# Attention outputs and gates of a fused transformer stretch by token instead of by feature, with a turn per tile

## The chip, the cores and the metric

One core of one Trainium2 chip runs the whole kernel in one launch. The metric is the device time in microseconds, as the median of three runs. A core has TensorE (matrix products, results in PSUM), VectorE, ScalarE, GpSimd and SyncE (here the queue that issues the loads), each with its own instruction stream; they meet at semaphores.

## The reference, cut to what matters

A batch of one, 256 tokens, width 2048, all in float32. First a layer with two token mixers, whose results are gated and added, then a feed-forward net; then two more layers (a pooling layer and a sparse attention layer), each with a small attention to a memory. The parts that the change touches:

```
# token mix
o = gla_chunked(q, k, v, log_a)                       # 4 heads, 512 values each
o = rmsnorm(o, gla_onorm_g) * silu(p_g)               # over the 512 of a head
y_gla = o @ gla_wo                                    # 2048 x 2048
y_mla = o_m @ mla_wo                                  # 2048 x 2048
merged = sigmoid(p_ga) * y_gla + sigmoid(p_gb) * y_mla
out = merged @ w_out
# pool layer
mixed = einsum('bsgc,gcd->bsgd', pooled, w_pool)      # 4 groups, 384 x 384
y_pool = mixed * scale * silu(zu)
y_mem = memory_attention(qm, mem, ...) * silu(zm)     # 4 heads
x + concatenate([y_pool, y_mem]) @ w_out
```

p_g, p_ga and p_gb are slices of h @ w_in, 2048 columns each.

## The kernel before

**Products.** Every large product runs as tiles of 512 output columns by 256 tokens. A tile needs its 2048 inputs in four pieces of weights (1 MB each, four chunks of 128 input rows by 512 columns). A piece is loaded into one of four w_raw buffers by SyncE's queue, which waits until the piece four places earlier has been used (free_slot). ScalarE rounds it to fp32r in two halves (w_hi, L1427), VectorE subtracts to get the rest (w_lo, L1843, also in two halves); the two together are called a cut. The cut of a piece may start when TensorE is done with the piece two places earlier, since there are two w_hi and two w_lo. TensorE then makes three passes, w_hi with x_hi, w_lo with x_hi, w_hi with x_lo (L945).

**Two modes.** In mode T the weights are stationary (128 x 128 blocks) and the 256 tokens move: the result stands by feature, [128 features, chunks, 256 tokens], and a piece is 48 matmuls of 256 columns. In mode N the tokens are stationary (two blocks of 128) and 512 weight columns move: the result stands by token, [128 tokens, 2, 512], and a piece is 24 matmuls of 512 columns. A product's input must stand by feature in either mode. Before, gla_g, gate_a, gla_wo, gate_b and mla_wo are in mode T; w_out, both parts of the feed-forward net and gla_v are in mode N.

**Order.** Each engine's stream is written out by its own product() calls, in the order gla_g, gate_a, gla_wo, mla_cq, mla_ckv, mla_kr, gate_b, the softmax attention, mla_wo, w_out. PSUM has two tile buffers (tile_ps) that alternate, and two for other work (misc_ps). A tile is emptied by ScalarE or VectorE (its "take"); this is held back and issued after the cut of the second piece of the next tile (or at the product's end). The list `between` gives extra steps, one after each piece. Products with rider=2 also carry the matrix ada_w: after each two pieces comes one ada piece, for which VectorE does four operations of 128x512 (L1914), and after two tiles TensorE sums them with eight matmuls. A piece of ada stands on VectorE ahead of the cut of the third and of the fifth piece from a tile's start. A product with several turns is a hardware loop on TensorE and SyncE, or has its first turn written out (peel), or is written out whole (flat).

**Around the linear attention.** Its output (gla_output, L1254) goes by feature into tile_ps[0], ScalarE copies it to qk (head_out, L1709). After the last head ScalarE squares all four heads, TensorE sums the squares over the features with 32 matmul instructions against ones (gla_sums), VectorE scales them, ScalarE takes the root, and VectorE the reciprocals of 128x1024 values in two steps (L2284). For each gla_g tile ScalarE makes Silu into gla_tmp, and VectorE (gated) multiplies four chunks by gain and reciprocal, multiplies by gla_tmp, and splits into o_hi and o_lo. gate_a becomes merged, gla_wo's take multiplies into it. mla_wo's take (both_merge) is four operations of 128x1024 on VectorE: times gate_b, plus merged, cast to h_hi, subtract to h_lo.

**The feed-forward net** already has the turn that the change brings elsewhere: a tile pair's result stands by token in o_tmp, eight transposes on TensorE (L1322) put it by feature into misc_ps[0], ScalarE rounds it, VectorE makes the low part.

**The pool stage.** pool_w has four pieces of three chunks by 384 columns, one per tile, cut over all 2048 columns of the buffer. The take of a tile (pool_take, L2439) makes three products, a cast and a subtraction on VectorE. The memory attention has nine steps over four units; the first three stand between the pieces of pool_w, the other six between those of pool_out, whose order has piece four of the first tile late. TensorE waits for all four takes before pool_out.

## Time and profile before

| | us |
|---|---|
| median of 3 runs (lowest, highest) | 2879.85 (2878.52, 2881.31) |
| the profiled execution | 2880.43 |
| its span, first to last instruction | 2878.6 |
| TensorE matmul busy | 2756.4 (96%) |
| VectorE busy | 1766.1 (61%) |
| ScalarE busy | 1220.8 (42%) |
| mean granted TensorE clock | 0.983 |

Busy times are of instructions, which overlap on TensorE: the spacing of two starts is shorter than the time of one matmul. Where starts are subtracted below, it is this spacing that counts.

### The profile page before, as it was taken

How to read it: one execution, taken by the hardware profiler on the slowest of the kernel's cores; microseconds unless marked ns; L12 is line 12 of the kernel's file. 1: busy time of each engine (PE TensorE's matmuls, PEld its weight loads, DVE VectorE, ACT ScalarE, POOL GpSimd, SP SyncE). 2: the span in 40 equal slices, each digit the busy share in tenths (PEclk: the TensorE clock that was granted, in tenths of full speed). 3: DMA queues.
4: the chain of work that ended last, by engine and by line, in shares of the span. 5: the costliest groups of instructions: out<-in, count | busy, mean ns of one | idle time of the engine just before them, and what ended most of it. 6: DMA issues, size and time to landing. Idle time of an engine off the chain costs nothing.

```text
span 2878.6 us, 41377 instructions
## 1 busy us (share of the span) xinstructions
PE 2756.4 (96%) x17422; PEld 2484.6 (86%) x17422; DVE 1766.1 (61%) x2132; ACT 1220.8 (42%) x1628; POOL 10.9 (0%) x21
## 2 busy tenths in 40 slices
PE   8989989999999999999999999999998999899998
PEld 6878878999999879888888888888997799899876
DVE  7866787767665567764445544456546556645765
ACT  6445433333434433444443343444443444434554
POOL 0000000000000000000000000000000000000000
PEclk9989999999999999999999999999999999999999
DMA  9987805877777247755555555554554545555233
GB/s 340 367 284 262 293 34 181 292 268 270 228 259 191 93 138 261 284 190 187 192 187 191 198 192 187 205 192 138 188 176 156 186 147 183 181 183 161 89 109 126
DMA packets 316861, 574.84 MB, mean 200 GB/s; under 512 B 22399, under 2 KB 61639, under 8 KB 315288
## 3 DMA queue, kind: packets, MB, share of 16 engines
q1 hardware_dynamic: 314034, 561.56, 57.4%
q0 software_dynamic: 2192, 10.77, 1.1%
q8 instruction: 122, 2.00, 0.3%
q14 instruction: 43, 0.35, 0.0%
q10 hardware_dynamic: 470, 0.16, 0.0%
HBM read 568.24 MB, written 4.21 MB: 199 GB/s over the span
## 4 chain that ended last, share of the span: by engine, by line
PE 82%; DVE 11%; DMA 3%; ACT 3%; issue 2%; SPq 0%; ACTq 0%; DVEq 0%
PE tile_ps L945 75%; PE misc_ps L945 6%; DVE w_lo L1843 4%; DMA w_raw<-in_w_mem_kv 2%; ACT w_hi L1427 1%; DVE probs_t L1914 1%; DVE probs_t L1934 1%; DMA w_raw<-in_w_in 1%; DVE strip_wide L1934 1%; PE misc_ps L1113 1%; PE misc_ps L1322 0%; DVE stats L2134 0%; DMA w_raw<-in_ada_w 0%; ACT mem_t L1640 0%; DVE gla_var L2284 0%
## 5 line engine op out<-in xcount | busy, mean ns | idle before, releaser
L1843 DVE TENSOR_TENSOR w_lo<-w_raw,w_hi 128x1024 fp32r<-128x1024 f32 x866 | 1020.9, 1221 | 903.9 <-ACT w_hi L1427 902.8
L1427 ACT ACTIVATE w_hi<-w_raw 128x1024 fp32r<-128x1024 f32 x866 | 868.6, 1051 | 1209.9 <-PE tile_ps L945 1150.7
L945 PE MATMUL tile_ps<-h_hi,w_hi 128*128 128x256 f32 x2544 | 429.6, 290 | 34.1 <-DVE w_lo L1843 18.8
L945 PE MATMUL tile_ps<-h_hi,w_lo 128*128 128x256 f32 x2544 | 420.3, 286 | 0.0
L945 PE MATMUL tile_ps<-h_lo,w_hi 128*128 128x256 f32 x2544 | 420.0, 286 | 0.0
L945 PEld LDWEIGHTS tile_ps<-h_hi,w_hi 128*128 128x128 f32 x2544 | 360.7, 195 | 42.1 <-issue 23.4
L945 PEld LDWEIGHTS tile_ps<-h_lo,w_hi 128*128 128x128 f32 x2544 | 359.3, 195 | 0.0
L945 PEld LDWEIGHTS tile_ps<-h_hi,w_lo 128*128 128x128 f32 x2544 | 359.2, 195 | 0.0
L945 PE MATMUL tile_ps<-w_hi,h_hi 128*128 128x512 f32 x1056 | 329.0, 393 | 5.4 <-DVE w_lo L1843 4.6
L945 PE MATMUL tile_ps<-w_lo,h_hi 128*128 128x512 f32 x1056 | 325.8, 390 | 0.0
L945 PE MATMUL tile_ps<-w_hi,h_lo 128*128 128x512 f32 x1056 | 325.7, 390 | 0.0
L945 PEld LDWEIGHTS tile_ps<-w_hi,h_hi 128*128 128x128 f32 x1056 | 196.8, 188 | 46.5 <-DVE w_lo L1843 6.2
L945 PEld LDWEIGHTS tile_ps<-w_lo,h_hi 128*128 128x128 f32 x1056 | 198.5, 188 | 41.7
L945 PEld LDWEIGHTS tile_ps<-w_hi,h_lo 128*128 128x128 f32 x1056 | 198.5, 188 | 41.6
L1914 DVE SCALAR_TENSOR_TENSOR probs_t<-w_raw,c_act,probs_t 128x512 f32<-128x512 f32 x240 | 180.1, 750 | 6.9
L945 PE MATMUL tile_ps<-w_hi,sw_hi 128*128 128x512 f32 x352 | 108.6, 390 | 0.0
L945 PE MATMUL tile_ps<-w_lo,sw_hi 128*128 128x512 f32 x352 | 108.4, 389 | 0.0
L945 PE MATMUL tile_ps<-w_hi,sw_lo 128*128 128x512 f32 x352 | 108.3, 389 | 0.0
L945 PE MATMUL tile_ps<-w_hi,o_hi 128*128 128x512 f32 x256 | 81.1, 398 | 10.7 <-DVE o_lo L1980 9.1
L945 PE MATMUL tile_ps<-o_hi,w_hi 128*128 128x256 f32 x512 | 83.9, 287 | 5.4 <-DVE w_lo L1843 4.2
L945 PE MATMUL tile_ps<-o_hi,w_lo 128*128 128x256 f32 x512 | 83.5, 286 | 0.0
L945 PE MATMUL tile_ps<-o_lo,w_hi 128*128 128x256 f32 x512 | 83.1, 285 | 0.0
(370 smaller groups left out, 2816.8 us busy)
## 6 DMA issues: line engine op xcount, KB each, us to landing
w_raw<-in_w_in SPq DMA_DIRECT2D x89, 1024.0 KB, 5.0
w_raw<-in_ffn_w_in SPq DMA_DIRECT2D x88, 1024.0 KB, 4.9
w_raw<-in_ada_w SPq DMA_DIRECT2D x80, 1024.0 KB, 5.1
w_raw<-in_w_out SPq DMA_DIRECT2D x48, 1024.0 KB, 5.1
w_raw<-in_ffn_w_down SPq DMA_DIRECT2D x44, 1024.0 KB, 5.0
w_raw<-in_b_w_in SPq DMA_DIRECT2D x33, 1024.0 KB, 5.3
w_raw<-in_a_w_in SPq DMA_DIRECT2D x32, 1024.0 KB, 5.3
w_raw<-in_w_kv SPq DMA_DIRECT2D x24, 1024.0 KB, 5.0
```

What stands on the lines that cost most here:

```text
L945: return nc.tensor.matmul(o, l, r, start=start, stop=stop, skip_group_check=True)
L1113: last = nc.tensor.transpose(bank[2][0:k, a * P:(a + 1) * P], probs_of(name, u0 + e)[:, hd * nk + j * P:hd * nk + j * P + k], ident)
L1427: f(w_hi[s_ % 2][:, hf], w_raw[r % 4][:, hf], ACT.Copy).then_inc(cut_hi, 1)
L1843: ins = v.tensor_tensor(w_lo[s_ % 2][:, hf], w_raw[r % 4][:, hf], f32(w_hi[s_ % 2][:, hf]), ALU.subtract)
L1914: ins = v.scalar_tensor_tensor(acc, w[:, c, :], c_act[:, k:k + 1], acc, ALU.mult, ALU.add)
L1934: ins = v.scalar_tensor_tensor(acc, w[:, c, :], c_act[:, k:k + 1], acc, ALU.mult, ALU.add)
```

## The change

Five products go to mode N, two of them flat. The linear attention's output is made by token, and its mean square comes from ScalarE as it empties PSUM. The gate (without the gain) is applied by token in place; each head is then turned back by eight transposes into misc_ps[0], where ScalarE (four operations with the gain as scale) and VectorE (four) make o_hi and o_lo. Both merges work by token; mla_wo's sum is turned back per tile in the same way, with one operation on each engine behind it. The turn of the last head or tile stands in the next product. In the pool stage the attention steps all stand in pool_out, in six groups of 2, 2, 2, 1, 1, 1; pool_out waits for each take where its chunk needs it; and a cut covers only the columns in use.

```diff
-            Product("gla_g", 4, 4, rider=2), Product("gate_a", 4, 4, rider=2),
-            Product("gla_wo", 4, 4, rider=2),
+            Product("gla_g", 4, 4, mode="N", rider=2, flat=True), Product("gate_a", 4, 4, mode="N", rider=2),
+            Product("gla_wo", 4, 4, mode="N", rider=2),
...
-            Product("gate_b", 4, 4, rider=2)]
+            Product("gate_b", 4, 4, mode="N", rider=2)]
...
-PRODUCTS += [Product("mla_wo", 4, 4, rider=2), Product("w_out", 4, 4, mode="N", rider=2)]
+PRODUCTS += [Product("mla_wo", 4, 4, mode="N", rider=2, flat=True), Product("w_out", 4, 4, mode="N", rider=2)]
...
+        MEM_A_GROUPS = (2, 2, 2, 1, 1, 1)
+        def in_next_tile(steps, at_, last_at):
+            out = [None] * BLK
+            for do in steps[:-1]:
+                out += [None] * at_ + [do] + [None] * (BLK - 1 - at_)
+            return out, [None] * last_at + [steps[-1]]
+        def halves(s_):
+            n = USED[s_] // 2
+            return slice(0, n), slice(n, 2 * n)
...  TensorE: linear attention output, sums, turns
-                for c in range(BLK):
-                    v = slice(hd * GLA_DV + c * P, hd * GLA_DV + (c + 1) * P)
-                    mm(tile_ps[0][:, c * S:(c + 1) * S], gla_v[:, 0, v], att[:, 0:2, :], c % 2 == 0, False)
-                    last = mm(tile_ps[0][:, c * S + P:(c + 1) * S], gla_v[:, 1, v], att[:, 2, :], False, True)
+                mm(tile_ps[0][:, 0:NT], att[:, 0, :], gla_v[:, 0, cs], True, True)
+                mm(tile_ps[0][:, NT:], att[:, 1, :], gla_v[:, 0, cs], True, False)
+                last = mm(tile_ps[0][:, NT:], att[:, 2, :], gla_v[:, 1, cs], False, True)
-            product("gla_g", *h, peel=True, between=[lambda: (pe.wait_ge(gl_out, GLA_H), gla_sums())])
+            def turn_tile(src, into):
+                for c in range(BLK):
+                    for tt in range(TT):
+                        last = nc.tensor.transpose(into[:, c * S + tt * P:c * S + tt * P + P],
+                                                   src[:, tt, c * P:c * P + P], ident)
+                return last
+            def turn_head(hd):
+                pe.wait_ge(gl_gated, TT * hd + TT)
+                if hd:
+                    pe.wait_ge(gl_ready, hd)
+                turn_tile(o_rows[:, hd], misc_ps[0]).then_inc(gl_turned, 1)
+            woven, last = in_next_tile([lambda hd=hd: turn_head(hd) for hd in range(GLA_H)], 0, 0)
+            product("gla_g", *h, between=woven)
+            product("gate_a", *h, between=last, peel=True)
+            product("gla_wo", *o, chunk_ready=lambda k: [(gl_ready, k // BLK + 1)] if k % BLK == 0 else [])
...
+            def turn_merged(tb):
+                pe.wait_ge(wo_merged, tb + 1)
+                if tb:
+                    pe.wait_ge(wo_ready, tb)
+                turn_tile(mla_tmp[:], misc_ps[0]).then_inc(wo_turned, 1)
+            woven, last = in_next_tile([lambda tb=tb: turn_merged(tb) for tb in range(BLK)], 1, 1)
+            product("mla_wo", *o, ready=fin("mla1"), between=woven)
...  ScalarE
+                for tt in range(TT):
+                    act.wait_ge(nm_sq, N["gla"].a0 + TT * hd + tt)
+                    f(sq_out[:], tile_ps[0][:, tt * NT:(tt + 1) * NT], ACT.Square,
+                      accum_out=row_sq[:, 0, tt, hd:hd + 1]).then_inc(nm_sq, 1)
+                f(o_rows[:, hd], tile_ps[0][:].rearrange("p (a b) -> p a b", a=TT), ACT.Copy).then_inc(gl_out, 1)
...
+            def head_high(hd):
+                act.wait_ge(gl_turned, hd + 1)
+                for c in range(BLK):
+                    f(o_hi[:, BLK * hd + c, :], misc_ps[0][:, c * S:(c + 1) * S], ACT.Copy,
+                      scale=vec("gla_onorm_g", c)).then_inc(gl_high, 1)
+            woven, last = in_next_tile([lambda hd=hd: head_high(hd) for hd in range(GLA_H)], 1, 1)
+            product("gla_g", silu_g, between=[gla_root] + woven[1:])
...  VectorE
+                for tt in range(TT):
+                    o_ = o_rows[:, hd, tt, :]
+                    v.scalar_tensor_tensor(o_, o_, row_sq[:, 1, tt, hd:hd + 1], gla_tmp[:, hd % 2, tt * NT:(tt + 1) * NT],
+                                           ALU.mult, ALU.mult).then_inc(gl_gated, 1)
...
-                step(i, tb, g, 0, v.tensor_tensor(t, in_chunks(ps[:]), some(gate_b, i, tb, g), ALU.mult))
-                step(i, tb, g, 1, v.tensor_tensor(t, t, some(merged, i, tb, g), ALU.add))
-                split_to(i, tb, g, 2, t, some(h_hi, i, tb, g), some(h_lo, i, tb, g), tk)
+                v.tensor_tensor(mla_tmp[:], ps[:].rearrange("p (t n) -> p t n", t=TT), gate_b[:, :, cs], ALU.mult).then_inc(tk, 1)
+                dve.wait_ge(taken[t_ % 2], t_ // 2 + 1)
+                v.tensor_tensor(mla_tmp[:], mla_tmp[:], merged[:, :, cs], ALU.add).then_inc(wo_merged, 1)
...  pool stage, TensorE
-            mem_a = attention_steps("mem_a")
-            product("pool_w", ..., between=[None, lambda: (mem_a_ready(), mem_a[0]()), mem_a[1], mem_a[2]])
-            all_taken(pe, G["pool_w"])
-            product("pool_out", *o, chunk_ready=mem_chunk("mem_a"), between=mem_a[3:])
+            mem_a = in_groups(attention_steps("mem_a"), MEM_A_GROUPS)
+            product("pool_w", ...)
+            def pooled_or_mem(k):
+                if k >= DC - MEM_H:
+                    return fin("mem_a") if k == DC - MEM_H else []
+                t = G["pool_w"].t0 + k // 3
+                return [(taken[t % 2], t // 2 + 1)] if k % 3 == 0 else []
+            product("pool_out", *o, chunk_ready=pooled_or_mem,
+                    between=[lambda: (mem_a_ready(), mem_a[0]())] + mem_a[1:])
```

## Rows read from the trace of the kernel before

**Rows 1.** The page: busy time (share) and instructions, then the chain that ended last.

```profile
PE 2756.4 (96%) x17422; PEld 2484.6 (86%) x17422; DVE 1766.1 (61%) x2132; ACT 1220.8 (42%) x1628; POOL 10.9 (0%) x21
...
PE 82%; DVE 11%; DMA 3%; ACT 3%; issue 2%; SPq 0%; ACTq 0%; DVEq 0%
```

**Rows 2.** Busy us in stretches; then granted clock, DMA share, GB/s.

```profile
core 0: us, PE busy (x) PEld busy (x) DVE busy (x) ACT busy (x) POOL busy (x), PEclk, DMA share, GB/s
476.00:478.60 2.60, 2.60 (x14) 2.60 (x13) 2.53 (x4) 0.00 (x0) 0.00 (x0) 0.50 1.05 404
428.00:541.00 113.00, 104.90 (x820) 103.29 (x819) 78.79 (x87) 42.26 (x42) 0.48 (x1) 0.97 0.59 210
541.00:635.00 94.00, 93.92 (x784) 93.72 (x784) 63.56 (x67) 36.96 (x38) 0.23 (x1) 1.00 0.81 288
1039.00:1141.00 102.00, 97.48 (x785) 96.88 (x785) 73.55 (x78) 30.73 (x31) 0.10 (x1) 0.97 0.69 241
1141.00:1232.00 91.00, 89.46 (x398) 73.27 (x399) 71.47 (x75) 37.07 (x46) 0.46 (x1) 1.00 0.81 287
1300.00:1523.00 223.00, 223.00 (x1010) 185.16 (x1008) 105.78 (x90) 90.05 (x91) 0.00 (x0) 1.00 0.56 189
2174.00:2202.70 28.70, 16.87 (x125) 15.36 (x125) 23.50 (x35) 14.19 (x20) 1.05 (x2) 0.88 0.61 218
```

**Rows 3.** Who waited for whom, TensorE, 428 to 1145: total, times, longest.

```profile
PE tile_ps L945 <- DVE w_lo L1843: 18.5, 9, 4.0
```

**Rows 4.** Timeline of TensorE in gla_g: start, us, instruction, [idle before <-releaser].

```profile
474.83 0.75 PE L945 MATMUL tile_ps<-h_hi,w_hi 128*128 128x256 f32 x4 [3.95 <-DVE w_lo L1843]
```

**Rows 5.** Timeline of TensorE: mode T, gate_a's first matmuls and its second half.

```profile
540.87 0.72 PE L945 MATMUL tile_ps<-h_hi,w_hi 128*128 128x256 f32 x4
...
588.16 0.72 PE L945 MATMUL tile_ps<-h_hi,w_hi 128*128 128x256 f32 x4
...
634.30 0.95 PE L945 MATMUL misc_ps<-const,probs_t 128*128 128x1 f32 x8
```

**Rows 6.** Timeline of TensorE: mode N in ffn_in, between two turns.

```profile
1299.99 1.03 PE L1322 MATMUL misc_ps<-const,o_tmp 128*128 128x128 f32 x8
1300.78 0.70 PE L945 MATMUL tile_ps<-w_hi,h_hi 128*128 128x512 f32 x2
...
1344.44 1.03 PE L1322 MATMUL misc_ps<-const,o_tmp 128*128 128x128 f32 x8
```

**Rows 7.** Timeline of TensorE: the sums of the linear attention's squares.

```profile
433.93 7.07 PE L945 MATMUL misc_ps<-gla_sq,const 128*128 128x256 f32 x32
```

**Rows 8.** Groups of instructions, 541 to 635: busy us, mean ns, idle before.

```profile
L1843 DVE TENSOR_TENSOR w_lo<-w_raw,w_hi 128x1024 fp32r<-128x1024 f32 x32 | 37.8, 1221 | 26.4 <-ACT w_hi L1427 26.4
...
L1427 ACT ACTIVATE w_hi<-w_raw 128x1024 fp32r<-128x1024 f32 x32 | 32.2, 1052 | 53.3 <-PE tile_ps L945 53.3
```

**Rows 9.** Timeline of VectorE in mla_wo: the take of a tile, then ada.

```profile
1067.40 1.22 DVE L2330 TENSOR_TENSOR mla_tmp<-tile_ps,gate_b 128x1024 f32<-128x1024 f32 x1
...
1069.91 0.69 DVE L1979 CAST h_hi<-mla_tmp 128x1024 fp32r<-128x1024 f32 x1
...
1071.78 3.11 DVE L1914 SCALAR_TENSOR_TENSOR probs_t<-w_raw,c_act,probs_t 128x512 f32<-128x512 f32 x4
```

**Rows 10.** Timeline of TensorE: first matmuls of mla_wo and of w_out.

```profile
1039.37 1.22 PE L945 MATMUL tile_ps<-o_hi,w_hi 128*128 128x256 f32 x4 [1.25 <-DVE o_lo L2119]
...
1140.97 0.71 PE L945 MATMUL tile_ps<-w_hi,h_hi 128*128 128x512 f32 x2
```

**Rows 11.** Timeline of ScalarE: a head's copy; a square of 512 columns in w_out.

```profile
404.75 1.03 ACT L1709 ACTIVATE qk<-tile_ps 128x1024 f32<-128x1024 f32 x1 [3.82 <-PE tile_ps L945]
...
1171.27 0.61 ACT L1549 ACTIVATE sq_out<-x 128x512 bf16<-128x512 f32 x1
```

**Rows 12.** Timeline of TensorE: the last scores in pool_w, pool_out's start.

```profile
2192.55 1.03 PE L945 MATMUL misc_ps<-mem_k,mem_q 128*128 128x256 f32 x4
2202.70 1.19 PE L945 MATMUL tile_ps<-w_hi,o_hi 128*128 128x512 f32 x2 [9.12 <-DVE o_lo L1980]
```

**Rows 13.** Timeline of VectorE: the products of a pool_w tile's take.

```profile
2181.28 1.26 DVE L2439 SCALAR_TENSOR_TENSOR pool_tmp<-tile_ps,cols,silu_z 128x256 f32<-128x256 f32 x3
```

More of the change, by code:

```diff
@@ L295 @@
     _k += _g.sums != "shared"
-    _a += {"pairs": _g.n // 2, "rows": 16 if _g.name == "pool" else 8, "shared": 0, "heads": GLA_H}[_g.sums]
-    _m += {"pairs": _g.n // 2, "rows": 0, "shared": 0, "heads": 1}[_g.sums]
+    _a += {"pairs": _g.n // 2, "rows": 16 if _g.name == "pool" else 8, "shared": 0, "heads": GLA_H * TT}[_g.sums]
+    _m += {"pairs": _g.n // 2, "rows": 0, "shared": 0, "heads": 0}[_g.sums]
     _c += _g.n * _g.split
@@ L310 @@
     _a += _w
-STEPS = {"gla_g": 2, "mla_wo": 3, "pool_w": 2}
+STEPS = {"pool_w": 2}
 STEP0 = {}
@@ L657, in do_next, with in_groups @@
                 return
+        def in_groups(steps, sizes):
+            at_ = [sum(sizes[:k]) for k in range(len(sizes))]
+            assert sum(sizes) == len(steps)
+            return [lambda a=a, n=n: [do() for do in steps[a:a + n]] for a, n in zip(at_, sizes)]
+        MEM_A_GROUPS = (2, 2, 2, 1, 1, 1)
         def by_fours(steps, n):
@@ L1732, in silu_g @@
                     act.wait_ge(gl_red, 2 * GLA_H)
-                f(gla_tmp[:, tb % 2, :], ps[:], ACT.Silu).then_inc(silu_ready, 1)
-            product("gla_g", silu_g, between=[None, gla_root])
-            product("gate_a", copy_to(chunks(merged), ACT.Sigmoid))
+                if tb >= 2:
+                    act.wait_ge(gl_gated, TT * (tb - 1))
+                f(gla_tmp[:, tb % 2, :], ps[:], ACT.Silu).then_inc(tk, 1)
+            def head_high(hd):
[5 more added lines that the diff above has]
+            product("gla_g", silu_g, between=[gla_root] + woven[1:])
+            product("gate_a", copy_to(columns(merged), ACT.Sigmoid), between=last)
             product("gla_wo")
@@ L1744, in _ @@
             norm("ckv")
-            product("gate_b", copy_to(chunks(gate_b), ACT.Sigmoid, pre=[(taken[b], (G["gla_g"].t1 - b + 1) // 2) for b in range(2)]))
+            product("gate_b", copy_to(columns(gate_b), ACT.Sigmoid, pre=[(gl_turned, GLA_H)]))
             for hf in range(2):
@@ L1752, in _, with merged_high @@
                 attention(f"mla{hf}")
-            product("mla_wo")
-            product("w_out", later=squares("ffn"))
+            def merged_high(tb):
+                act.wait_ge(wo_turned, tb + 1)
+                f(h_hi[:, BLK * tb:BLK * tb + BLK, :], misc_ps[0][:].rearrange("p (a b) -> p a b", a=BLK),
+                  ACT.Copy).then_inc(wo_high, 1)
+            woven, last = in_next_tile([lambda tb=tb: merged_high(tb) for tb in range(BLK)], 2, 1)
+            product("mla_wo", between=woven)
+            product("w_out", between=last, later=squares("ffn"))
             norm("ffn")
@@ L1789, in _ @@
             product("pool_zm", copy_to(lambda i, tb, g: mem_z[:, :, :], ACT.Silu))
-            mem_a = attention_steps("mem_a")
-            product("pool_w", between=[None] + mem_a[0:3])
-            product("pool_out", later=squares("kv"), between=mem_a[3:] + [lambda: tables(1)])
+            mem_a = in_groups(attention_steps("mem_a"), MEM_A_GROUPS)
+            product("pool_w")
+            product("pool_out", later=squares("kv"), between=mem_a + [lambda: tables(1)])
             norm("kv")
@@ L2298, in _, with gla_roots @@
-            product("gla_g", gated, between=[None, gla_mean, lambda: gla_roots(0), lambda: gla_roots(1)])
-            product("gate_a")
+            def gla_roots():
+                dve.wait_ge(nm_sq, n_gla.a0 + TT * GLA_H)
+                if n_gla.k:
+                    dve.wait_ge(nm_std, n_gla.k)
+                v.tensor_scalar(row_sq[:, 1], row_sq[:, 0], 1.0 / GLA_DV, EPS, ALU.mult, ALU.add).then_inc(nm_var, 1)
+                dve.wait_ge(nm_std, n_gla.k + 1)
+                own.wait(v.reciprocal(row_sq[:, 1], row_sq[:, 1]))
@@ L2301, in gla_merge @@
+            product("gla_g", gated, between=[gla_roots] + woven[1:])
+            product("gate_a", between=last)
             def gla_merge(i, tb, g, ps, tk):
                 tile_is_done(dve, g, i, tb)
-                m = some(merged, i, tb, g)
-                v.tensor_tensor(m, m, in_chunks(ps[:]), ALU.mult).then_inc(tk, 1)
+                m = merged[:, :, bass.ds(per(i, g.body * NT) + tb * NT, NT)]
+                v.tensor_tensor(m, m, ps[:].rearrange("p (t n) -> p t n", t=TT), ALU.mult).then_inc(tk, 1)
@@ L2368, in residual @@
                 return take
-            product("w_out", residual("w_out", gated=True))
+            product("w_out", residual("w_out", gated=True), between=last)
             norm("ffn")
@@ L2445, in _ @@
             dve.wait_ge(pl_lo, 1)
[L2446 to L2448 removed]
+            mem_a = in_groups(attention_steps("mem_a"), MEM_A_GROUPS)
+            product("pool_w", pool_take)
+            product("pool_out", residual("pool_out"), between=mem_a + [lambda: tables(1)])
             norm("kv")
```

92 lines of the change are left out of this document (37 added, 55 removed).

## The prediction

> **What bounds the kernel now.** I read the page first. TensorE is busy for 96% of the span and holds 82% of the chain that ended last; VectorE has 11% of that chain [rows 1]. So a gain has to come out of TensorE's stream: fewer nanoseconds for the same columns, fewer instructions, or shorter stalls. The windows by stage come next [rows 2]. In 541 to 635 (gate_a) TensorE is busy 93.9 of 94 us at a granted clock of 1.00: nothing but the stream itself costs time there. In 428 to 541 (gla_g) it is 104.9 of 113, in 1039 to 1141 (mla_wo) 97.5 of 102, both at clock 0.97, and in 2174 to 2202.7 (pool_w) 16.9 of 28.7 at 0.88: there it waits. The reader should then look at who is waited for: between 428 and 1145 it is VectorE's cut of the next weight piece, 18.5 us in nine waits [rows 3]. After the wait of 3.95 us that ends at 474.83 the stream also runs slower for a while: in 476 to 478.6 the granted clock is 0.50, the lower of the two levels (1.2 of 2.4 GHz) [rows 2, 4]. That costs about half of some 3 us, 1.5 us more.
>
> **The two forms of a piece.** Five products (gla_g, gate_a, gla_wo, gate_b, mla_wo; 80 pieces of four chunks) go from 48 matmuls of 256 columns a piece to 24 of 512; the columns are the same. What the form costs is in two stretches without a stall. Eight pieces in the old form: 588.16 to 634.30, 46.14 us, 5.77 a piece [rows 5]. Eight in the new form, in ffn_in: 1300.78 to 1344.44, 43.66 us, 5.46 a piece [rows 6]. So 0.31 us a piece, 2.48 for eight, 24.8 for the 80. This is 120 ns for 256 columns against 227 for 512. The Trainium skill (TensorE: Matmul & The Clock Gate, Back-to-back issue gap) speaks against this term: it gives N/2.4 + 2.5 ns for a matmul alone, 109 and 216 ns. By it a piece would shrink from 5.24 to 5.18 us only, and the 80 pieces would give an estimated 5 us. The rows measure both forms in this kernel and both lie above that rule, the short one by more; I go by the rows.
>
> Each of the four heads of gla_g and the four tiles of mla_wo is turned back on TensorE: eight transposes, 0.79 us from 1299.99 to 1300.78 [rows 6], 0.87 with the bubble at the switch. The ada sum after two tiles stays: eight small matmuls, 0.95 us in its row, 0.81 of the stream [rows 5].
>
> **gla_g, now 112.8 us** (428.1, the start of its window, to 540.87 [rows 2, 5]). New: 2 x 43.66 + 2 x 0.81 + 3 turns x 0.87 = 91.55. The sums of squares by matmul go: 32 matmuls, 7.07 us busy, 6.8 of the stream [rows 7]; ScalarE makes them while it empties PSUM. Do stalls come back? I walk one tile, counted from the end T of its fourth piece. ScalarE cuts a piece in 2.0 us, VectorE in 2.36, one behind the other half by half [rows 8]: the cut of the next tile's second piece is ready at T+3.4. Then VectorE gates the head, two operations of 128x512, about 0.75 each like the four of ada at 3.11 [rows 9]: T+4.9, before the turn is wanted at T+5.46. The ada piece follows to T+8.0 and the cut of the third piece to T+10.4; it is wanted at T+11.8. Then ScalarE rounds the turned chunks (four of 128x256) and VectorE makes the low parts, about 1.8 us, with 2 us to spare before the next cut. So no stall in the steady state. At the start ScalarE has the new squares, the copy and the root with its table, and VectorE waits for them before the ada piece: cut of the third piece at about T0+10.4, wanted at T0+10.9. The first Silu has a table load of some 1.3 us before it, so the first turn waits about 0.6. Together 92.15: **-20.6**. Of this, 5.0 is the form, 6.8 the sums, the rest the stalls and the slow clock behind them, less the turns. VectorE's two reciprocals over 512 elements become one over eight.
>
> **gate_a**: the form, -5.0, the fourth turn +0.87, a stall of 0.3 in its first half gone: **-4.4**. **gla_wo** -5.0. **gate_b** -5.0. Their takes keep their size, and their loads ask for no more than w_out's, which run at 287 GB/s in the new form with the same riders [rows 2].
>
> **mla_wo, now 101.6 us** (1039.37 to 1140.97 [rows 10]). VectorE's take of a tile is four operations, 1067.40 to 1071.78, 4.4 us, then ada 3.11 and the next cut [rows 9]: at T+3.4+4.4+3.0+2.4 = T+13.2, wanted at T+11.5, which is one of the nine stalls. New: two operations, 2.45 us. The third piece's cut is then ready at T+11.4 and wanted, behind the turn, at T+11.8. Tight but not late. 2 x 43.66 + 1.62 + 3 x 0.87 = 91.55, plus 1.3 for the clock that is low after the attention before it: 92.8, **-8.8**. **w_out** gets the last turn, +0.87, and loses the wait of 0.6 for the old long take; the two waits of 0.7 behind its residuals stay: **+0.2**.
>
> **The linear attention's own loop.** Its output matmuls have the same number of columns. ScalarE's emptying of a head was one copy of 1.03 us; now two squares of 0.61 with their sums (about 0.75 each in all) come first [rows 11]. The decay's exponential stands behind it, and TensorE's next decay behind that. VectorE was the tightest there, with about 1 us of cover for these. I take 0.3 for each of three heads, **+1.0**; the bounds are 0 and 3 x 1.5 = 4.5.
>
> **The pool stage.** Now the first piece of pool_out starts at 2202.70, after a wait of 9.12 us for VectorE's last low part; its start also runs at the lower clock, 1.7 us lost [rows 12]. VectorE has four takes of 2.85 us (1.26 for the products of 2181.28 and the rest for a cast and a low part over 768 elements) [rows 13], the cuts, and three attention steps mixed in, which also hold up ScalarE's cuts. New: no attention in pool_w, cuts of the 1152 used columns instead of 2048 (about 1.4 us instead of 2.36), and pool_out's first piece needs only the third take, not the fourth. Walked: second piece at 2177.7; takes 0 and 1 end at 2182.7 and 2187.0 and each frees the PSUM tile that the piece two on waits for; first full cut to 2189.5; third take to 2192.4. pool_out starts at 2192.4, 10.3 earlier, and 1.7 of slow clock goes. Against it the three pairs of scores, which lay in stalls, now stand in the stream (four matmuls, 0.85 of the stream each, 2.55) [rows 12], and two steps at once make TensorE wait inside a group (0.3 and 0.9 us, estimated by walking the steps): 10.3 + 1.7 - 2.55 - 1.2 = **-8.2**. Bounds 0 and -12.
>
> **Sum.** -20.6 - 4.4 - 5.0 - 5.0 - 8.8 + 0.2 + 1.0 - 8.2 = -50.8. The profiled execution took 2880.4 us (span 2878.6), 0.6 above the median of 2879.85; 2880.4 - 50.8 = 2829.6. I forecast **2829.5**.
>
> **Rivals.**
> (a) The turn is a new handshake between three engines with one PSUM buffer; two of its margins are 0.4 us. If each of the eight turns ends in a late cut as the nine waits do now (mean 2.05 us, half of them with 1.5 us of low clock), that is 8 x 2.8 = 22 us: 2852. For it: VectorE is at 70% in these stages already. Against: ffn_in weaves the same turn and TensorE is busy 223.0 of 223 us there [rows 2], though without ada pieces. 12%.
> (b) The pool stage only moves its waits: the packed attention steps stall pool_out by what pool_w saves, 2838. For it: two steps of one group depend on each other across the engines. 8%.
> (c) The new form gives nothing beside riders, and pieces stay at 5.77 us: 2829.6 + 24.8 = 2854. Against it [rows 6]; w_out, with riders, takes 91 us for its 16 pieces and the waits named. The rule of the Trainium skill weighed above would come near this case. 1%.
> (d) Slower: the clock falls to its lower level in the new stretches. A matmul of 512 columns would then take some 0.43 us instead of 0.227, a piece 4.9 us more, so 11 of the 80 pieces at the lower level eat the whole gain, and all 80 would give about 3220 us. Against: ffn_in with five turns and w_out with riders both stand at 1.00 [rows 2]; 2%. The Trainium skill (the same page, PE-mode transpose) says that transposes do not count as busy time for the clock, which would be the way into this case; in 1300 to 1523 the trace shows 40 transposes or more and no fall, so it does not agree at this density.
>
> **Chances.** Forecast 77%, its own range 2822 to 2838 (bounds of the loop and of the pool stage); (a) 12, (b) 8, (c) 1, (d) 2. The range of eight in ten: 2819 to 2846. What a measurement can tell from no change is about 0.2%, 5.8 us: faster 97%, same 1% (a partial (d)), slower 2%.
>
> **What would show it.** TensorE's spacing for two matmuls of 512 columns in gate_a 0.455 us, not 0.48; gla_g about 92 us, gate_a 90, gla_wo 89, mla_wo 93; no wait for VectorE's cut over 1 us in gla_g after its first tile; pool_out's first matmul some 18 us behind pool_w's first instead of 28. I am wrong if waits for w_lo in these products sum to over 8 us, or if pool_out's first five pieces take more than 37 us.

## The result: 2831.4 us against 2829.5 forecast, and the profile after

| | before | changed |
|---|---|---|
| median, us (lowest to highest) | 2880.58 (2878.52 to 2881.82), 4 runs | 2831.43 (2829.57 to 2832.07), 4 runs |
| profiled execution, its span | 2880.43, 2878.6 | 2831.92, 2830.1 |

The ratio of the times is 0.9829, interval 0.9812 to 0.9846: 49.2 us saved, 50.8 forecast. The page of the changed kernel, to be held against [rows 1]: busy time and instructions, then the chain that ended last.

```profile
PE 2726.1 (96%) x15494; PEld 2374.0 (84%) x15494; DVE 1745.1 (62%) x2123; ACT 1228.0 (43%) x1660; POOL 10.9 (0%) x21
...
PE 87%; DVE 7%; ACT 3%; DMA 2%; issue 1%; SPq 0%; ACTq 0%; DVEq 0%
```

TensorE's records hold 1928 fewer matmuls and it is busy 30 us less; the other 18 us were idle time. Its share of the chain rose and VectorE's fell from 11% to 7%. By stage, the stretches that answer to [rows 2] (gla_g, gate_a, gla_wo, mla_wo, w_out, pool_w; the columns are the same):

```profile
429.40:522.00 92.60, 92.09 (x427) 76.32 (x425) 67.11 (x82) 43.04 (x54) 0.37 (x1) 1.00 0.71 253
522.00:611.80 89.80, 89.80 (x411) 74.69 (x410) 63.48 (x70) 38.64 (x42) 0.34 (x1) 1.00 0.85 303
611.80:700.70 88.90, 88.90 (x403) 73.89 (x402) 64.44 (x68) 33.02 (x34) 0.00 (x0) 1.00 0.81 286
1009.10:1102.20 93.10, 93.06 (x424) 77.45 (x425) 71.02 (x74) 33.42 (x34) 0.08 (x1) 0.98 0.75 260
1102.20:1193.70 91.50, 90.42 (x411) 74.57 (x410) 71.08 (x74) 38.00 (x47) 0.48 (x1) 1.00 0.84 291
2135.80:2154.10 18.30, 13.83 (x111) 13.05 (x109) 14.64 (x23) 8.87 (x12) 1.05 (x2) 1.00 0.82 274
```

TensorE is now busy in all but 0.5 us of the first four, and VectorE does more in each microsecond than before and is hardly waited for. TensorE's waits there, as in [rows 3] (for whom: us in total, times, longest); the first line is 429 to 701, the others 1009 to 1194. Of the nine waits for w_lo of [rows 3], 18.5 us, seven are gone: the four of gla_g (8.1 us) and the three of mla_wo (4.2). The other two stay, in gate_b's stretch (2.26, now 2.68) and at the start of the softmax attention (4.02 in both). w_out keeps two of 0.54 of its three.

```profile
PE misc_ps L1300 <- DVE o_rows L2344: 0.5, 1, 0.5
...
PE tile_ps L967 <- DVE w_lo L1897: 1.1, 2, 0.5
PE tile_ps L967 <- DVE o_lo L2173: 1.0, 1, 1.0
```

TensorE's timeline in the changed kernel: the first turn, then gate_a's second tile pair, eight pieces between two ada sums.

```profile
457.64 1.09 PE L1300 MATMUL misc_ps<-const,o_rows 128*128 128x128 f32 x8 [0.51 <-DVE o_rows L2344]
458.49 0.70 PE L967 MATMUL tile_ps<-w_hi,h_hi 128*128 128x512 f32 x2
...
566.08 0.62 PE L967 MATMUL tile_ps<-w_hi,h_lo 128*128 128x512 f32 x2
566.53 0.95 PE L967 MATMUL misc_ps<-const,probs_t 128*128 128x1 f32 x8
567.35 0.71 PE L967 MATMUL tile_ps<-w_hi,h_hi 128*128 128x512 f32 x2
...
610.98 0.95 PE L967 MATMUL misc_ps<-const,probs_t 128*128 128x1 f32 x8
```

From 567.35 to 610.98 are 43.63 us; [rows 5] had 46.14 for the same work and [rows 6] 43.66. Two matmuls of 512 columns take 566.53 - 566.08 = 0.45 us.

**Where the time came from.** Each stretch runs from TensorE's first matmul of the stage to that of the next, in the two profiled executions (us).

| stretch | before | changed | difference | forecast |
|---|---|---|---|---|
| start to gla_g | 428.10 | 429.34 | +1.24 | +1.0 |
| gla_g | 112.77 | 92.64 | -20.13 | -20.6 |
| gate_a | 94.24 | 89.81 | -4.43 | -4.4 |
| gla_wo | 93.91 | 88.88 | -5.03 | -5.0 |
| mla_cq to its norm | 47.94 | 47.94 | 0 | 0 |
| mla_ckv, mla_kr, gate_b | 110.31 | 107.57 | -2.74 | -5.0 |
| softmax attention | 152.10 | 152.96 | +0.86 | 0 |
| mla_wo | 101.60 | 93.06 | -8.54 | -8.8 |
| w_out | 91.37 | 91.47 | +0.10 | +0.2 |
| feed-forward net and on, to pool_w | 942.07 | 942.09 | 0 | 0 |
| pool_w | 28.29 | 18.33 | -9.96 | |
| pool_out | 104.87 | 107.56 | +2.69 | -8.2 for both |
| the rest | 570.99 | 568.45 | -2.54 | 0 |
| sum | 2878.56 | 2830.10 | -48.46 | -50.8 |

Two rows missed: gate_b's by 2.3 and the rest by 2.5, in opposite directions. The rest is unchanged code. The windows of the sparse attention, first before, then changed:

```profile
2650.00:2700.00 50.00, 47.24 (x365) 44.71 (x364) 34.49 (x95) 27.61 (x84) 0.00 (x0) 0.97 0.27 85
2700.00:2740.00 40.00, 37.85 (x288) 35.62 (x287) 30.48 (x84) 21.12 (x67) 0.00 (x0) 0.96 0.23 79
```

```profile
2604.00:2654.00 50.00, 47.23 (x377) 44.70 (x376) 36.00 (x96) 28.08 (x84) 0.00 (x0) 1.00 0.27 86
2654.00:2694.00 40.00, 37.85 (x301) 35.62 (x300) 31.81 (x90) 20.72 (x66) 0.00 (x0) 1.00 0.25 81
```

The granted clock is 0.97 and 0.96 against 1.00. From the first matmul behind pool_out to the last of all, these two took 558.62 and 556.12, and the eleven experiments, which don't change this stage either, 554.8 to 559.2. So it is no gain of the change: the granted clock differed between executions of the same code.

Other stretches differ in the same way, and a difference of 1 to 3 us in such a row can't be read from one pair of executions. gate_a and gla_wo repeat to 0.04 us (89.77 to 89.81, and 88.88), but the old mla_wo took 101.60 here and 104.53 in pool_only (below), which doesn't touch it; the new gla_g 92.6 or 93.2 to 93.5; the stretch with gate_b 105.9 to 106.0 in four executions, 107.4 to 107.6 in three and 105.2 in one; the new pool_out 107.5 or 109.1 to 109.2; the new loop of the linear attention 70.0 in two and 70.8 to 70.9 in the others.

**What lies behind gate_b.** TensorE around the norm of mla_ckv in the changed kernel, and VectorE beside it:

```profile
759.30 3.49 PE L967 MATMUL misc_ps<-nscratch_o,const 128*128 128x256 f32 x8 [2.95 <-ACT nscratch_o L1545]
762.23 1.21 PE L967 MATMUL tile_ps<-w_hi,h_hi 128*128 128x512 f32 x2
...
776.56 1.12 PE L967 MATMUL tile_ps<-w_hi,h_hi 128*128 128x512 f32 x2 [2.68 <-DVE w_lo L1897]
777.48 1.05 PE L967 MATMUL tile_ps<-w_lo,h_hi 128*128 128x512 f32 x2
```

```profile
765.52 2.36 DVE L1897 TENSOR_TENSOR w_lo<-w_raw,w_hi 128x1024 fp32r<-128x1024 f32 x2
767.80 0.88 DVE L2116 SCALAR_TENSOR_TENSOR ntmp_o<-ckv,cols,rstd 128x256 f32<-128x256 f32 x2
...
771.91 2.33 DVE L1968 SCALAR_TENSOR_TENSOR probs_t<-w_raw,c_act,probs_t 128x512 f32<-128x512 f32 x3
774.15 4.62 DVE L1897 TENSOR_TENSOR w_lo<-w_raw,w_hi 128x1024 fp32r<-128x1024 f32 x4
```

VectorE does the cut, the norm's chunks (767.8 to 771.4), ada and the next cut in a row. TensorE had this wait before too, 2.26 us. It ends when VectorE ends, so the two shorter pieces ahead of it only make it longer. The sums of 759.30 also ran at the lower clock here: eight matmuls 3.49 us, where before's took 1.99 behind the same wait of 2.94. In after_again (below) these sums took 1.99 too, the wait was 2.85, and the stretch 106.00 instead of 107.57. So 1.6 of the 2.3 us that this row missed are the low clock of one execution; 0.6 us (2.85 - 2.26) are the gain of the form in the two pieces ahead of the wait, 2 x 0.31, spent in it.

### The profile page after: what moved, and what is told of

Same layout as the page of the kernel before. It is cut to its first block, busy times and chain, and to the rows that moved or that the text cites. A ratio compares the mean times of both kernels' runs of the same rounds, so it can differ in the third digit from the quotient of the medians.

```text
span 2830.1 us, 37311 instructions
## 1 busy us (share of the span) xinstructions
PE 2726.1 (96%) x15494; PEld 2374.0 (84%) x15494; DVE 1745.1 (62%) x2123; ACT 1228.0 (43%) x1660; POOL 10.9 (0%) x21
## 4 chain that ended last, share of the span: by engine, by line
PE 87%; DVE 7%; ACT 3%; DMA 2%; issue 1%; SPq 0%; ACTq 0%; DVEq 0%
PE tile_ps L967 79%; PE misc_ps L967 7%; DVE w_lo L1897 2%; ACT w_hi L1465 1%; DMA w_raw<-in_w_in 1%; DMA w_raw<-in_w_mem_kv 1%; DVE probs_t L1988 1%; PE misc_ps L1135 0%; DVE stats L2188 0%; PE misc_ps L1353 0%; DVE probs_t L1968 0%; ACT mem_t L1678 0%; PE misc_ps L1300 0%; DVE strip_wide L1988 0%; DVE nsa_probs L2184 0%
## 5 line engine op out<-in xcount | busy, mean ns | idle before, releaser
L967 PE MATMUL tile_ps<-w_hi,h_hi 128*128 128x512 f32 x1440 | 450.0, 394 | 8.0 <-DVE w_lo L1897 7.2
L967 PE MATMUL tile_ps<-w_hi,h_lo 128*128 128x512 f32 x1440 | 444.6, 390 | 0.0
L967 PE MATMUL tile_ps<-w_lo,h_hi 128*128 128x512 f32 x1440 | 444.5, 390 | 0.0
L967 PE MATMUL tile_ps<-h_hi,w_hi 128*128 128x256 f32 x1776 | 301.5, 289 | 25.5 <-DVE h_lo L2247 9.2
L967 PE MATMUL tile_ps<-h_lo,w_hi 128*128 128x256 f32 x1776 | 294.5, 285 | 0.0
L967 PE MATMUL tile_ps<-h_hi,w_lo 128*128 128x256 f32 x1776 | 294.0, 285 | 0.0
L967 PEld LDWEIGHTS tile_ps<-h_hi,w_hi 128*128 128x128 f32 x1776 | 251.7, 194 | 32.1 <-issue 22.2
L967 PEld LDWEIGHTS tile_ps<-h_hi,w_lo 128*128 128x128 f32 x1776 | 250.3, 194 | 0.0
L967 PE MATMUL tile_ps<-w_lo,o_hi 128*128 128x512 f32 x512 | 158.3, 390 | 0.0
L967 PE MATMUL tile_ps<-w_hi,o_lo 128*128 128x512 f32 x512 | 158.2, 390 | 0.0
```

Of the source, the lines that this page charges most:

```text
L967: return nc.tensor.matmul(o, l, r, start=start, stop=stop, skip_group_check=True)
```

## The experiments

Their times are medians beside runs of the kernel before on the same chip; the stretches come from each profiled execution. The unchanged version of the changed kernel came out at 2832.23 in its second set (after_again, below); totals are held against 2831.4 to 2832.2. The edits are cut to what matters; where two engines have the same edit, one is shown.

**pool_only: the kernel before with the new pool stage alone.**

```diff
-            mem_a = attention_steps("mem_a")
-            product("pool_w", between=[None] + mem_a[0:3])
-            product("pool_out", later=squares("kv"), between=mem_a[3:] + [lambda: tables(1)])
+            mem_a = in_groups(attention_steps("mem_a"), MEM_A_GROUPS)
+            product("pool_w")
+            product("pool_out", later=squares("kv"), between=mem_a + [lambda: tables(1)])
```

> The kernel before with the pool part of the change alone: attention steps in pool_out in groups, takes waited for where needed, cuts of the used columns. In the changed kernel's trace the stretch from pool_w's first matmul to the first matmul behind pool_out is 7.3 us shorter. Theory (the two parts are independent): 2880.5 - 7.3 = 2873, the same stretch 125.9 us. Rival (the pool stage profits from, or is paid by, the mix stage before it): over 2877 or under 2870.

Measured 2872.78 (2868.31 to 2877.91, six runs), ratio 0.997 (0.9958 to 0.9983): 8.0 saved, the total as expected. pool_w took 18.32, pool_out 109.12, together 127.4 where 125.9 was expected. The latter is 1.56 more than in the changed kernel with the same code, and the first 5 us of pool_out show why, first pool_only, then the changed kernel:

```profile
2198.00:2203.00 5.00, 4.96 (x15) 3.94 (x16) 4.48 (x7) 1.17 (x1) 0.00 (x0) 0.66 0.36 139
```

```profile
2154.10:2159.10 5.00, 5.00 (x22) 4.11 (x23) 4.90 (x7) 1.12 (x1) 0.00 (x0) 1.00 0.33 129
```

Clock 0.66 against 1.00, 15 matmuls against 22. Both have the same wait of 2.27 us ahead of them. Of the eight profiles that have this wait, three show the low clock behind it (pool_only, long_take, short_turn). The forecast had counted 1.7 us for a low clock that would go; it goes in some executions only.

**mix_only: the changed kernel with the old pool stage and whole cuts.**

```diff
-            n = USED[s_] // 2
+            n = 1024
...
-            mem_a = in_groups(attention_steps("mem_a"), MEM_A_GROUPS)
-            product("pool_w")
-            product("pool_out", later=squares("kv"), between=mem_a + [lambda: tables(1)])
+            mem_a = attention_steps("mem_a")
+            product("pool_w", between=[None] + mem_a[0:3])
+            product("pool_out", later=squares("kv"), between=mem_a[3:] + [lambda: tables(1)])
```

> The changed kernel with the pool stage as before. Theory: 2831.4 + 7.3 = 2839, every stretch of the token mix as in the changed kernel. Rival: the gains of the two parts overlap, and the sum of the two parts' gains differs from the whole by over 3 us.

2841.95 (2834.27 to 2844.7), ratio 0.9856 (0.9838 to 0.9875): 38.9 saved, 3 us fewer than expected, with four runs that lie 10 us apart. With pool_only's 8.0 that is 46.9 of the 49 of both together; the 2.3 between are under the 3 us named for the rival. That the parts don't touch each other is shown to within that. The stretches of the token mix are those of after_again to 0.2 us. pool_w is back at 28.28, and TensorE's wait ahead of pool_out at 9.12, to the hundredth that of [rows 12].

**three_in_t: gate_a, gla_wo and gate_b back in mode T.**

```diff
-Product("gate_a", 4, 4, mode="N", rider=2)   (gla_wo and gate_b too)
+Product("gate_a", 4, 4, rider=2)
```

> The changed kernel, but gate_a, gla_wo and gate_b move 256 tokens again (their results are then taken as if they stood by token, so the output is not the reference's). It prices the form alone, with riders and no change in takes. Theory (a matmul of 512 columns costs less than two of 256, 0.31 us a piece): gate_a and gla_wo +5.0 each, gate_b +2.7 since part of it is hidden by a stall that ends when VectorE is done: 2831.4 + 12.7 = 2844. Rival (the form is worth nothing, the gain came from shorter takes alone): 2831.

2842.57 (2841.11 to 2845.5), ratio 0.9869 (0.9852 to 0.9885). gate_a took 94.78 (+4.97) and gla_wo 93.90 (+5.02). TensorE, eight pieces of gate_a in this run:

```profile
571.10 0.72 PE L967 MATMUL tile_ps<-h_hi,w_hi 128*128 128x256 f32 x4
...
617.25 0.95 PE L967 MATMUL misc_ps<-const,probs_t 128*128 128x1 f32 x8
```

46.15 us against 43.63, nothing else being different: the form's term is shown, 2.5 us for eight pieces with riders too, and rival (c) is out. gate_b's stretch took 110.28. Against the first profile of the changed kernel (107.57) that is the +2.7 that was expected, but the agreement is luck: there the norm's sums ran at the low clock, here at the full one. Against after_again (106.00), with the full clock in both, it is +4.3, 14 pieces of 0.31 us. The gain of the other two goes into the wait for VectorE's cut; first this run, then after_again:

```profile
786.35 1.23 PE L967 MATMUL tile_ps<-h_hi,w_hi 128*128 128x256 f32 x4 [2.26 <-DVE w_lo L1897]
```

```profile
779.11 1.22 PE L967 MATMUL tile_ps<-w_hi,h_hi 128*128 128x512 f32 x2 [2.85 <-DVE w_lo L1897]
```

By the rule of the Trainium skill weighed in the prediction (TensorE: Matmul & The Clock Gate, Back-to-back issue gap), which that section gives for a matmul alone, these 48 pieces would have lost an estimated 3 us. The stretches lost 14.3 us against executions with the same clock (5.0, 5.0 and 4.3), so the trace does not agree.

**long_take: VectorE has two idle operations more in mla_wo's take.**

```diff
                 v.tensor_tensor(mla_tmp[:], mla_tmp[:], merged[:, :, cs], ALU.add).then_inc(wo_merged, 1)
+                own.wait(v.tensor_tensor(mla_pad[:], gate_b[:, :, 0:NT], gate_b[:, :, 0:NT], ALU.mult))
+                own.wait(v.tensor_tensor(mla_pad[:, 0], gate_b[:, 0, 0:NT], gate_b[:, 0, 0:NT], ALU.mult))
```

> The changed kernel with two idle operations (128x1024 and 128x512, about 2.0 us) added to VectorE's take of each mla_wo tile, so that the take is as long as before the change; their result is used by nobody. Theory (the stalls were VectorE's take, ada piece and cut in a row, and the margin is 0.4 us): the cut of the third piece of tiles 1 to 3 comes 1.6 us late, and one more cut in w_out: 4 x 1.6 = 6 us and up to 1.5 of slow clock for some of them, mla_wo 98 to 101 us instead of 93.1, total 2838 to 2840. Rival (the old stalls came from the form, or from the loads): mla_wo stays at 93, total 2831.

2835.7 (2835.02 to 2837.36), ratio 0.9845 (0.9828 to 0.9861). mla_wo took 97.42 instead of 93.06. VectorE, then TensorE, in this run:

```profile
1034.49 1.22 DVE L2391 TENSOR_TENSOR mla_tmp<-tile_ps,gate_b 128x1024 f32<-128x1024 f32 x1
1035.74 1.23 DVE L2393 TENSOR_TENSOR mla_tmp<-mla_tmp,merged 128x1024 f32<-128x1024 f32 x1
1036.88 1.22 DVE L2394 TENSOR_TENSOR mla_pad<-gate_b 128x1024 f32<-128x1024 f32 x1
1038.14 0.69 DVE L2395 TENSOR_TENSOR mla_pad<-gate_b 128x512 f32<-128x512 f32 x1
1038.86 3.11 DVE L1969 SCALAR_TENSOR_TENSOR probs_t<-w_raw,c_act,probs_t 128x512 f32<-128x512 f32 x4
1041.89 4.62 DVE L1898 TENSOR_TENSOR w_lo<-w_raw,w_hi 128x1024 fp32r<-128x1024 f32 x4
```

```profile
1044.30 0.50 PE L968 MATMUL tile_ps<-w_hi,o_hi 128*128 128x512 f32 x1 [1.52 <-DVE w_lo L1898]
```

The take grew by 1.9 to 2.0 us and TensorE waits 1.52: the margin was 0.4 to 0.5 us, the forecast's T+11.4 against T+11.8. In all 3.4 us of waits for w_lo come back in mla_wo (three: 1.5, 0.3, 1.5) and one of 0.5 in w_out. That is less than the 98 to 101 us and the total of 2838 to 2840 that were expected, since the middle wait is short and no low clock followed any of them (1.00 in the 5 us behind each). The direction and the place are as expected: an old take of 4.4 us stalls mla_wo in the new form too, by the row take, ada, cut.

**short_turn: one transpose of eight in each turn.**

```diff
-                for c in range(BLK):
-                    for tt in range(TT):
+                for c in range(1):
+                    for tt in range(1):
```

> The changed kernel with one transpose instead of eight in each of the eight turns, all waits kept (the rest of the turned tile is stale, so the output is not the reference's). Theory (a turn costs its 0.79 us in the stream and nothing by its waits): each turn 0.69 us shorter, 5.5 in all: 2826. But the turn is also the cover for the cut behind it, with 0.4 us to spare in mla_wo: up to 0.3 us of it may come back as a stall there in three tiles. Rival (the handshake itself costs, several us): the total hardly moves or the gaps around the one transpose stay over 1 us.

2828.74 (2827.06 to 2830.65), ratio 0.9816 (0.98 to 0.9832). gla_g 91.07, gate_a 89.04, mla_wo 90.48, w_out 90.74. gate_a and w_out, with one turn each, lost 0.77 and 0.73. The four stretches are 5.65 below the changed kernel's first profile, but the clock has a part in that: the first 5 us of gla_g ran at 0.86 here and at 1.00 there, those of mla_wo at 1.00 here and at 0.69 there. Against executions with nearly the same clock (long_take's gla_g, 93.24; three_in_t's mla_wo, 91.67) the three turns of each are worth 2.2 and 1.2, so the eight are worth 4.9: the 5.5 expected, less two waits of 0.3. The total fell by 2.7 to 3.5, less than the 5.5 expected; the profiled execution reached gla_v at 274.13, the latest of all. The turn is paid in full on TensorE, and it also gives VectorE time. Without it the cut is late by what was left:

```profile
1042.84 0.73 PE L967 MATMUL tile_ps<-w_hi,o_hi 128*128 128x512 f32 x2 [0.30 <-DVE w_lo L1897]
```

**squares_later: ScalarE empties a head with one copy and squares it a round later from SBUF.**

```diff
-                for tt in range(TT):
-                    f(sq_out[:], tile_ps[0][:, tt * NT:(tt + 1) * NT], ACT.Square, ...)
                 f(o_rows[:, hd], tile_ps[0][:]..., ACT.Copy).then_inc(gl_out, 1)
+            def head_squares(hd):
+                act.wait_ge(gl_out, hd + 1)
+                for tt in range(TT):
+                    f(sq_out[:], o_rows[:, hd, tt, :], ACT.Square, ...)
...
+                    if e % 2 and k % 2 and k > 1:
+                        head_squares(k // 2 - 1)
```

> The changed kernel, but ScalarE copies a head out of PSUM first and squares it from SBUF one round later, behind the next decays. Theory (the 1.2 us lost in the linear attention's loop are the squares, 1.5 us a head, in front of the decays): the loop ends 1 us earlier, gla_g starts at 428.3 instead of 429.3; but the last head's squares now come behind its copy, with no change for the root: total 2830.5. Rival (the loss is a slow-clock or load effect): gla_g starts at 429.3 as before.

2825.7 (2825.22 to 2826.93), ratio 0.9806 (0.979 to 0.9822). In the changed kernel a head was emptied by this (ScalarE; 419.41 to 421.73), with TensorE behind it:

```profile
419.41 0.60 ACT L1749 ACTIVATE sq_out<-tile_ps 128x512 bf16<-128x512 f32 x1 [3.75 <-PE tile_ps L967]
419.90 0.19 ACT L1749 ACTIVATION_READ_ACCUMULATOR sq_out<-tile_ps 128x1 f32 x1
...
420.72 1.01 ACT L1751 ACTIVATE o_rows<-tile_ps 128x1024 f32<-128x1024 f32 x1
```

```profile
421.79 0.49 PE L967 MATMUL tile_ps<-q_lev,k_across 128*128 128x128 f32 x2 [0.63 <-ACT o_rows L1751]
```

With the copy first that wait is gone. The loop, from its first decay matmul to gla_g's first matmul, took 68.91 before, 70.01 changed (70.82 in after_again) and 68.40 here. So the loop's term is shown: +1.1 to +1.9, where most of the 0.8 between is the low clock of the last head's output matmuls (4.14 us in after_again, 2.84 in the first profile), and the cure is worth 1.6 to 2.4. The total fell by 5.7, more than the loop explains. The spans of the two profiled executions differ by 5.0: 1.6 in the loop, 2.4 in gate_b's stretch (105.19; its sums took 2.68 us instead of 3.49 and no low clock followed its wait), 0.8 in the softmax attention and 0.5 ahead of gla_v, with 0.3 lost elsewhere. The edit touches only the loop; the other code is the same.

**scores_in_stalls: two pairs of scores back between pool_w's pieces**, on TensorE alone.

```diff
-            mem_a = in_groups(attention_steps("mem_a"), MEM_A_GROUPS)
+            steps = attention_steps("mem_a")
+            mem_a = [None] + in_groups(steps[2:], MEM_A_GROUPS[1:])
             product("pool_w", ...,
+                    between=[None, lambda: (mem_a_ready(), steps[0]()), None, steps[1]])
...
-                    between=[lambda: (mem_a_ready(), mem_a[0]())] + mem_a[1:])
+                    between=mem_a)
```

> The changed kernel, but TensorE makes the first two pairs of scores between the pieces of pool_w, where it waits 1.5 and 2.3 us for VectorE; VectorE's and ScalarE's steps stay in pool_out. Theory (these scores cost their 0.85 us each in pool_out's stream): the stretch from pool_w to the end of pool_out 1.7 us shorter, 124.2 instead of 125.9, total 2829.7. Rival (VectorE is the chain through the whole stage, so TensorE's work moved away changes nothing): 125.9.

2830.81 (2830.07 to 2833.7), ratio 0.9823 (0.9807 to 0.984). pool_w stayed at 18.33 and pool_out went from 107.56 to 105.98. Here is pool_out, this run and then the changed kernel (last row: from 2154 to 2262):

```profile
2154.40:2260.40 106.00, 102.49 (x469) 82.86 (x469) 63.06 (x87) 47.41 (x75) 0.54 (x1) 1.00 0.50 166
```

```profile
2154.00:2262.00 108.00, 104.56 (x479) 84.71 (x480) 63.49 (x89) 47.53 (x75) 0.54 (x1) 1.00 0.49 164
```

The clock is 1.00 in both, so the 1.6 us are the matmuls that now lie in a stall. The total, 2830.81, can't tell this from nothing.

**whole_cuts: a cut of pool_w over all 2048 columns again.**

```diff
-            n = USED[s_] // 2
+            n = 1024
```

> The changed kernel with cuts of all 2048 columns in pool_w, as before the change. VectorE's three remaining cuts there get 0.95 us longer each, ScalarE's 0.7. Theory (VectorE's row of cuts and takes sets pool_w): pool_out starts 2 to 2.9 us later, 20.3 to 21.2 us behind pool_w instead of 18.3; total 2833.5 to 2834.5. Rival (the takes alone set it): no change.

2835.01 (2833.34 to 2839.34), ratio 0.9837 (0.9821 to 0.9853). pool_w 19.84, +1.5, under the 2 to 2.9 expected of it: VectorE's cuts are part of the row that sets pool_w, but not all of their 0.95 us comes through. The rest of the total is not in the pool stage: this profiled execution reached gla_v at 273.30 and had 559.2 behind pool_out, both near the top of their ranges.

**after_again: the changed kernel once more.** It has no edit.

> The changed kernel once more, on the same chip as the next two, for the comparison with them. Theory: 2831, with the part before the linear attention scattering by some us from run to run, since it is the loads at the start that differ there.

2832.23 (2828.86 to 2834.35, five runs), ratio 0.9826 (0.9813 to 0.984). pool_out 107.52, as before; gate_b's stretch 106.00 instead of 107.57, because the norm's sums ran at full clock (eight matmuls, 1.99 us). gla_g took 93.45 instead of 92.64: its first 5 us ran at clock 0.83 here, and at 1.00 in the first profile.

**ckv_later: the norm's chunks of mla_ckv behind the cut of gate_b's third piece**, on ScalarE and VectorE.

```diff
-            norm("ckv")
-            product("gate_b")
+            sums("ckv")
+            cut_in_norm("ckv", -1)
+            product("gate_b", between=[None, None, lambda: apply("ckv", cuts=False)])
```

(VectorE's part; cuts=False leaves out a cut that apply would make.)

> The changed kernel, but the chunks of the second small norm (ckv) are made behind gate_b's third cut instead of ahead of its ada piece and cut. Theory (gate_b gained 2.7 us instead of 5.0 because VectorE's norm chunks stand in front of its first cut, so TensorE waits 2.7 us whatever the form): that wait goes, with the slow matmuls behind it; from the sums' first matmul to the softmax attention's first product 103 us instead of 106.0 to 107.6; total 2828. Rival (VectorE's work only moves into gate_b's later pieces and stalls them): 106 or more.

2827.79 (2824.26 to 2829.14), ratio 0.9808 (0.9793 to 0.9823). gate_b's stretch took 103.31, 2.7 less than after_again and 4.3 less than the changed kernel's first profile. TensorE:

```profile
787.19 0.74 PE L967 MATMUL tile_ps<-w_hi,h_hi 128*128 128x512 f32 x2 [1.62 <-DVE w_lo L1900]
```

The wait of 2.68 is gone, one of 1.62 stands two pieces on, and no low clock comes with it: over 770 to 800 the granted clock is 1.00, against 0.94 in the changed kernel. With this the stretch is 7.0 under before's, the 5.0 of the form and part of the old wait. The theory that stands with the expectation was half right: the wait and the slow matmuls behind it do go, but they had taken only 0.6 us of the form's gain (above). The rival has a part in it too, as the wait of 1.62 shows.

**all_four: squares_later, scores_in_stalls and ckv_later together**, and five matmuls on TensorE ahead of the norm's sums. Shown is what is new:

```diff
             product("mla_kr", *h)
+            for _ in range(5):
+                mm(bank[1], ident, const[:, 0:512], True, True)
             norm("ckv")
```

> The changed kernel with the squares later, the two pairs of scores in pool_w, the ckv chunks later, and five matmuls into an unused bank ahead of the ckv sums so that the clock stays up while TensorE waits for ScalarE. Theory, by the single runs: loop -2.0, pool stage -1.6, gate_b's stretch -3 to -4: 2831.4 - 7 = 2824, ratio to the changed kernel 0.9975. Rival (the parts meet: the gain of one is taken by the wait of the next): under 3 us in all.

2827.25 (2820.54 to 2830.48, five runs), ratio 0.9808 (0.9792 to 0.9824). Loop 68.40, gate_b's stretch 104.37, softmax attention 150.00, pool_out 106.00. TensorE's waits from 740 to 800:

```profile
PE tile_ps L967 <- DVE w_lo L1910: 1.6, 1, 1.6
PE misc_ps L967 <- ACT nscratch_o L1549: 0.8, 1, 0.8
```

The five matmuls cover the wait of 2.95 us but make the stretch 1.06 longer than in ckv_later; whether the attention's 150.00 (151.3 to 153.0 elsewhere) is theirs stays open. The first three gains are there by stretch. The median is 3 us above the 2824 expected and 5.0 below after_again's, on the same chip, yet the intervals of the two ratios touch (0.9813 and 0.9824), so by the total it isn't settled that it beats the changed kernel.

## Why the prediction was right, step by step

- **The form.** 0.31 us a piece: 43.63 against 46.14 for eight, in the changed kernel and, one edit alone, in three_in_t. It held in full where no stall stood behind it (gate_a, gla_wo).
- **gla_g**, -20.1 for -20.6. Its parts are read from the two traces, and no experiment takes them apart. Four waits for w_lo (0.87, 3.95, 1.07, 2.22 us) became one of 0.51 at the first turn (forecast 0.6): 7.6. The form gave 5.0 and the sums 6.8, the low clock behind two of the old waits an estimated 3 (some four groups of matmuls each, 0.85 us apart instead of 0.48), and the turns took 2.4. That makes 20.0. The granted clock is 1.00 over the stretch, so the slow phase behind [rows 4] went with the wait; seven of the other profiles have a clock of 0.83 to 0.89 in its first 5 us, behind the loop, and there the stretch is 0.6 to 0.8 longer.
- **The turn.** 0.85 from 457.64 to 458.49, 0.87 forecast; the margins of 0.4 us held in mla_wo, where long_take and short_turn both show how thin they are. Rival (a) needed eight late cuts; there was none in gla_g and mla_wo.
- **mla_wo**, -8.5 for -8.8. long_take brings a stall back by operations as long as those that the change took away. The old stretch also varies: in pool_only, with the same code, it took 104.53, with the low clock for longer at its start and behind its first wait of 1.77 us, which the first profile has at the full clock. Against that execution the gain is 11.3 to 11.5, so the close hit is partly luck.
- **The loop**, +1.2 for +1.0 with the start in it; it was +1.9 in most later executions, for the clock. The late decay that the forecast had named is there in the first two heads (393.66 to 396.85 between two k_across matmuls, 3.19 us, against 2.95 before and 2.93 in squares_later): 0.25 each. In the third head it is TensorE's own wait for the buffer, 0.63, which the forecast had not named.
- **The pool stage**, -7.3 for -8.2. pool_out starts 10.0 us earlier (10.3 forecast), and the waits inside the paired steps are 0.46 and 0.56 (0.3 and 0.9). The first five pieces of pool_out took 37.1 us, 2154.09 to 2191.23, a hair over the 37 named as the mark for "wrong": the steps between them cost 4.2 us more than before, not 3.75. It isn't rival (b), by which the whole stage would have gained nothing. That the low clock behind the old wait went (1.6 of the 7.3) is luck of this execution. TensorE, the two waits:

```profile
2176.73 0.66 PE L1135 MATMUL misc_ps<-const,probs 128*128 128x128 f32 x4 [0.46 <-DVE probs L2201]
...
2177.95 1.13 PE L967 MATMUL misc_ps<-probs_t,mem_v 128*128 128x128 f32 x8 [0.56 <-DVE o_lo L2173]
```

- **gate_b was mis-sized**, -2.7 for -5.0. The form was priced as in gate_a, without a walk of what VectorE does ahead of its third piece. There a wait ends when VectorE ends, so the gain of the two pieces ahead of it is lost (0.6 us), and -4.3 was to be had, as after_again's 106.00 shows. The other 1.6 us are the low clock in the sums ahead of it in this execution.
- **w_out**, +0.1 for +0.2. The old waits were 0.46 and twice 0.54, not 0.6 and twice 0.7; the two of 0.54 stayed, as forecast.
- **Rival (d)** fell too: clock 1.00 in gla_g, gate_a and gla_wo, with turns in the first two.

That the total came within 2 us owes something to chance: the unchanged rest gave 2.5 back, while the low clock in gate_b's sums took 1.6 and the unchanged softmax attention 0.9.

## What to carry to other kernels

Price another form of the same work from two stretches of one trace that have no wait in them, then walk the helper engine's row (take, rider, cut) in each product by itself: a gain in the pieces ahead of a wait for that engine isn't had (0.6 of 5.0 us in gate_b), and a margin of 0.4 us is worth knowing. Work that TensorE must do anyway costs nothing in its own waits and its full price anywhere else, as the scores show. Subtract stretches and not totals when an edit is worth 1 to 3 us of 2830, and only stretches whose granted clock is the same in both executions: in gate_b an expected +2.7 us was met here by a difference of clock, where the edit was worth +4.3.
